# Squares of three norms: added by GpSimd two tiles at a time, then two products with ones instead of eight

## What is computed

```
def rmsnorm(x, w):
    xf = x.astype(jnp.float32)
    y = xf * lax.rsqrt(jnp.mean(xf * xf, axis=-1, keepdims=True) + NORM_EPS)
    return (y * w.astype(jnp.float32)).astype(x.dtype)
...
    for i in range(DEPTH):
        h = rmsnorm(x, norm_mix[i])
        ...                                   # i = 0: gated linear attention, i = 1: attention
        x = x + conv_ffn(rmsnorm(x, norm_ffn[i]), ffn_w_up[i], ffn_w_conv[i],
                         ffn_b_conv[i], ffn_w_down[i])
    return x
```

## Time and profile before

| | us |
|---|---|
| median of 3 runs | 1097.27 (1096.15 to 1099.2) |
| the profiled execution | 1096.36 |
| its span, first to last instruction | 1094.2 |

### The profile page before, as it was taken

One profiled execution on the slowest core, in us unless ns is written; L12 is line 12 of the kernel. 1 busy time (PEld: TensorE's weight loads), 2 busy tenths in 40 slices (PEclk: granted clock), 3 DMA queues, 4 the chain that ended last, 5 costly groups with the idle time before them and its releaser, 6 DMA issues.

```text
span 1094.2 us, 25181 instructions
## 1 busy us (share of the span) xinstructions
PE 1049.2 (96%) x10822; PEld 997.4 (91%) x10822; DVE 834.3 (76%) x1372; ACT 614.0 (56%) x878; POOL 15.4 (1%) x32
## 2 busy tenths in 40 slices
PE   3999999999998999999999978999999999999997
PEld 2999999999998988999999978889999988889997
DVE  3964579878887775997888756789899899855573
ACT  4853565444445664654444457646568576676443
POOL 1000000000000000000000000000000000000000
PEclk9999999999999999999999989999999999999999
DMA  8462256766654422567665744433333232224531
GB/s 271 145 203 77 78 177 222 249 234 203 222 192 154 147 85 96 173 233 246 215 229 192 214 131 126 127 98 120 114 117 117 79 117 79 79 79 153 192 118 39
DMA packets 135431, 168.08 MB, mean 154 GB/s; under 512 B 2928, under 2 KB 124784, under 8 KB 134960
## 3 DMA queue, kind: packets, MB, share of 16 engines
q1 hardware_dynamic: 131632, 153.51, 43.5%
q0 software_dynamic: 3712, 13.31, 3.2%
HBM read 164.70 MB, written 2.10 MB: 152 GB/s over the span
## 4 chain that ended last, share of the span: by engine, by line
PE 86%; DVE 8%; ACT 3%; DMA 1%; issue 1%; SPq 0%; DVEq 0%; ACTq 0%
PE bank L310 18%; PE bank L311 16%; PE bank L312 16%; PE banks L619 2%; PE bank L623 2%; PE bank L621 2%; PE banks L623 2%; PE bank L619 2%; PE banks L621 2%; DVE hf L2408 2%; DMA consts<-in_consts 1%; PE bank L1129 1%; DVE wl L272 1%; PE banks L1097 1%; DVE wl L296 1%; PE bank L582 1%
## 5 line engine op out<-in xcount | busy, mean ns | idle before, releaser
L310 PE MATMUL bank<-xh,wh 128*128 128x256 f32 x1360 | 398.5, 293 | 0.6 <-DVE wl L272 0.6
L311 PE MATMUL bank<-xl,wh 128*128 128x256 f32 x1392 | 393.8, 283 | 0.0
L312 PE MATMUL bank<-xh,wl 128*128 128x256 f32 x1360 | 384.6, 283 | 0.0
L310 PEld LDWEIGHTS bank<-xh,wh 128*128 128x128 f32 x1360 | 260.1, 191 | 11.1 <-issue 4.1
L311 PEld LDWEIGHTS bank<-xl,wh 128*128 128x128 f32 x1392 | 266.7, 192 | 1.1 <-issue 1.0
L312 PEld LDWEIGHTS bank<-xh,wl 128*128 128x128 f32 x1360 | 260.3, 191 | 0.0
L272 DVE TENSOR_TENSOR wl<-raw,wh 128x2048 fp32r<-128x2048 f32 x96 | 218.9, 2286 | 50.3 <-ACT wh L267 50.1
L267 ACT ACTIVATE wh<-raw 128x2048 fp32r<-128x2048 f32 x96 | 182.8, 1906 | 38.6 <-PE bank L623 34.3
L296 DVE TENSOR_TENSOR wl<-raw,wh 128x1024 fp32r<-128x1024 f32 x86 | 103.7, 1217 | 23.2 <-ACT wh L288 23.1
L2408 DVE SCALAR_TENSOR_TENSOR hf<-big,vecs,hf 128x256 f32<-128x256 f32 x240 | 101.4, 477 | 0.0
L288 ACT ACTIVATE wh<-raw 128x1024 fp32r<-128x1024 f32 x86 | 87.6, 1057 | 11.2 <-PE bank L312 5.5
(11 more groups left out here) (394 smaller groups left out, 2207.1 us busy)
## 6 DMA issues: line engine op xcount, KB each, us to landing
raw<-in_ffn_w_up SPq DMA_DIRECT2D x44, 1024.0 KB, 5.1
raw<-in_w_in SPq DMA_DIRECT2D x36, 1024.0 KB, 5.5
raw<-in_ffn_w_down SPq DMA_DIRECT2D x22, 1024.0 KB, 5.1
raw<-in_gla_w_in SPq DMA_DIRECT2D x12, 1024.0 KB, 6.1
big<-in_ada_w_t POOLq DMA_DIRECT2D x24, 512.0 KB, 5.4
raw<-in_attn_w_qkv SPq DMA_DIRECT2D x6, 1024.0 KB, 5.0
raw<-in_gla_w_out SPq DMA_DIRECT2D x4, 1024.0 KB, 5.0
raw<-in_attn_w_out SPq DMA_DIRECT2D x4, 1024.0 KB, 5.1
```

The costliest lines, as they stand in the source:

```text
L310: nc.tensor.matmul(ps, wh, xh, start=start, stop=False)
L311: nc.tensor.matmul(ps, wh, xl, start=False, stop=False)
L312: return nc.tensor.matmul(ps, wl, xh, start=False, stop=stop)
```

## The change

For the three norms GpSimd adds the squares of the pairs 1, 2 and 3 to those of pair 0 in `HF[:, 0:2, :]`, one pair as soon as ACT has written it, each addition waiting for the one before. TensorE no longer issues ones products in m = 0 of `early_product`. It waits for the third addition behind the second group of three matmuls of m = 1 and there issues two products with ones. GpSimd's queue holds the additions of norm 1 ahead of the first modulation load, those of norm 2 ahead of load 12, and those of norm 3 ahead of load 14.

```
+            def squares_added(i):
+
+                for g in range(1, 4):
+                    pool.wait_ge(sem("squares_ready"), 4 * i + g + 1)
+                    if g > 1:
+                        pool.wait_ge(sem("squares_added"), 3 * (i - 1) + g - 1)
+                    ins = nc.gpsimd.tensor_tensor(HF[:, 0:2, :], HF[:, 0:2, :], HF[:, 2 * g:2 * g + 2, :], ALU.add)
+                    ins.then_inc(sem("squares_added"), 1)
+
             pool.wait_ge(sem("rms_split"), 4)
             pool.wait_ge(sem("gla_out_split"), GH_)
+            squares_added(1)
             pool.wait_ge(sem("rstd_ready"), 2)
             for j in range(MODS):
+                if j == MODS_FIRST:
+                    squares_added(2)
+                    pool.wait_ge(sem("attn_split"), QH)
+                if j == MODS_FIRST + 2:
+                    squares_added(3)
                 if j >= 3:
                     pool.wait_ge(sem("ada_summed"), j - 2)
-                if j == MODS_FIRST:
-                    pool.wait_ge(sem("attn_split"), QH)
...
-                        if m == 0 and k % 2:
-                            pe.wait_ge(sem("squares_ready"), 4 * i + k // 2 + 1)
-                            for kk in (k - 1, k):
-                                summed = nc.tensor.matmul(PS[3][:, 0:T], ones, HF[:, kk, :], start=kk == 0,
-                                                          stop=kk == KT - 1)
-                            if k == KT - 1:
-                                summed.then_inc(sem("square_sums"), 1)
+                        if m == 1 and k == 1:
+                            pe.wait_ge(sem("squares_added"), 3 * i)
+                            for kk in range(2):
+                                summed = nc.tensor.matmul(PS[3][:, 0:T], ones, HF[:, kk, :], start=kk == 0, stop=kk == 1)
+                            summed.then_inc(sem("square_sums"), 1)
```

## The result

The changed kernel took 1102.34 us (median of 5 runs, 1100.28 to 1103.97), the kernel before, run beside it, 1096.15 (1094.51 to 1099.2). The ratio is 1.0043, with a 95% interval of 1.0028 to 1.0057, so 4.7 us (3.1 to 6.2) are lost. The two medians are 6.2 us apart, and the measured one lies 2.3 us above the forecast; for gains and losses I go by the ratios and their intervals. The forecast was 2.75 us of loss, 1100.0 us, with a range of 1093.3 to 1104.5 that holds the measured time. The profiled execution has a span of 1100.2 us against 1094.2, 6.0 us more. I first give where these 6.0 lie; the experiments then show that two of the places need a second look.

The account below looks back on a forecast made before the run. TensorE was taken as the bound in norm 1, VectorE close behind or tight in the others. Losses of 0.15, 0.4 and 2.2 us made 2.75, added to the median 1097.3: 1100.0 us, range 1093.3 to 1104.5.

Parts of the forecast that it names:

- Turns decide: All three norms: GpSimd additions and VectorE's two-input SBUF instructions exclude each other; 2.75 us slower in sum, chance 0.48.
- starvation: Norms 1 and 3: GpSimd gets no turn while VectorE runs back to back; 6.9 us slower in all, chance 0.14.
- Rival 1: All three norms: the additions disturb nobody, VectorE's instructions keep their lengths; 3.7 us faster, chance 0.27.
- An addition: Duration of one GpSimd addition: 1.25 us, the middle by ratio of VectorE's 0.68 and 2.29 us.
- The second estimate: Duration of one GpSimd addition from the skill's ratio of 1.96 between GpSimd and VectorE: given as 1.35 us.
- GpSimd's wake: GpSimd starts late after the semaphore it waits for: 0.6 us.
- Norm 1: First norm: the third addition delays VectorE's splits by 1.25 us less 0.26 idle; the down product starts 0.15 us later.
- the free case: GpSimd disturbs nobody: gains of 1.1, 2.5 and 0.1 us in norms 1, 2 and 3, sum 3.7 us.
- Norm 2: Second norm: low parts alternate with additions, the last ending at 356.8 instead of 353.88; the product ends 0.4 us later.
- TensorE waits for VectorE in that stretch anyway: Norm 2, window 353 to 354 at 1.2 GHz: counted without cost; up to 2.9 us if it lasted through m = 1.
- Norm 3: Third norm: the three additions push VectorE by 2.35 us; the down product starts 2.2 us later.
- rival 3: Additions over 1.8 us, or 1.2 GHz through norm 2: 1 to 2 us on top of either case; chance 0.11.

Follow-up runs that it names:

- a2: The kernel before with the nine GpSimd additions beside it, written to spare tiles, TensorE keeping all its products; ratio 1.0029 to the kernel before, 3.2 us slower.
- a3: The changed kernel with GpSimd copying pairs of squares to spare tiles instead of adding, sums over pair 0 alone; ratio 0.9985 to the kernel before.
- a4: The changed kernel with GpSimd writing zeros to spare tiles instead of adding, sums over pair 0 alone; ratio 0.9975 to the kernel before.
- a1: The changed kernel without the additions, sums over pair 0 alone; ratio 0.9976 to the kernel before, 2.6 us faster.
- d1: The changed kernel with six of eight ones products put back into each norm as filling, additions kept; ratio 1.0032 to the kernel before.

## Why the prediction was right, and where it was not

- **Turns decide (the choice that no row proved).** Right, and shown by a2, a3 and a4. The engine that asks first is served at the end of the other's instruction; starvation is refuted, since the addition at 158.31 came while VectorE ran back to back, took 1.47 us, was served ahead of the splits, and RS was not late in norm 1. Rival 1, no disturbance, is refuted by a2.
- **An addition.** 1.25 us forecast, 1.28 measured, up to 2.69 with its own wait in it. The second estimate there, 0.68 x 1.96, is 1.33 and not 1.35; nothing hangs on it. GpSimd's wake was taken as 0.6 us from a DMA issue; in norms 2 and 3 the additions started 0.1 us after the squares.
- **Norm 1.** +0.15 forecast, 0.0 measured. The two splits grew by 1.10, and TensorE waited 0.68 us for the hidden tiles, as the prediction said it would. The gain of 1.1 in the free case was right too (a1: 25.36).
- **Norm 2.** +0.4 forecast against the earlier trace rows, +0.38 measured against the same rows. The agreement is luck, since two sizes were wrong and cancel. TensorE was to start pair 3 at 356.86 - 350.07 = 6.79 us into the norm, and started it after 5.95, as pair 1, which the prediction put off by a whole addition, was not held up at all. Behind it 4.46 us were to follow, and 5.30 did, the first part of them at 0.50:

```profile
358.89 0.58 PE L310 MATMUL bank<-early_hi,wh 128*128 128x256 f32 x1 [0.17 <-DVE early_lo L1920]
```

The baseline flatters too: the step "TensorE waits for VectorE in that stretch anyway" took the window at 0.50 as costless. It had cost 1.6 us of the 10.87. At equal clock the additions alone cost 10.51 - 9.25 = 1.3 us (a2), and without a drop the saving is 0.84 and not 2.5.
- **Norm 3.** +2.2 forecast, +2.76 measured. The turns alone are smaller than the forecast: +1.84 in a2 and +2.01 in d1, since early_lo's low parts grew by 0.2 + 1.65 and not by 2.35. The other 0.8 to 0.9 is the clock, which the sum had only for norm 2. TensorE made the sums at 1.2 GHz, and VectorE ran out of work for 0.69 us. VectorE, ScalarE and TensorE there after:

```profile
448.57 3.41 DVE L1920 SCALAR_TENSOR_TENSOR early_lo<-x,vecs,early_hi 128x256 fp32r<-128x256 f32 x4
451.91 4.48 DVE L272 TENSOR_TENSOR wl<-raw,wh 128x2048 fp32r<-128x2048 f32 x2
457.08 1.67 DVE L1907 SCALAR_TENSOR_TENSOR hf<-x,vecs,rs 128x256 f32<-128x256 f32 x4 [0.69 <-ACT rs L1309]
...
456.63 0.42 ACT L1309 ACTIVATE rs<-rs 128x256 f32<-128x256 f32 x1
...
454.17 1.91 PE L596 MATMUL bank<-hf,consts 128*128 128x256 f32 x4
```

The four low parts took 3.41 against 1.77. The four records of the sums took 1.91 us against 1.03 in the earlier trace rows.

The prediction also looked for new idle time of TensorE in front of the down products of norms 1 and 3. Norm 1 has it. In norm 3 of the change TensorE waits three times for a low part, 0.83, 1.35 and 0.85 us, and from the last of these waits on it runs to the down product without any. So there TensorE, slowed by the clock, was the last to be late, 0.3 us behind the hidden tiles. Without a drop, in a2, it does wait for them. First the last wait and the hidden tiles' low part of the change, then the down product of a2:

```profile
452.04 0.38 PE L310 MATMUL bank<-early_hi,wh 128*128 128x256 f32 x1 [0.85 <-DVE early_lo L1920]
...
474.47 0.69 DVE L2014 TENSOR_TENSOR gl<-big,gh 128x512 fp32r<-128x512 f32 x1 [0.76 <-ACT gh L1369]
```

```profile
474.35 0.35 PE L632 MATMUL banks<-gh,wh 128*128 128x256 f32 x1 [0.52 <-DVE gl L2017]
```

Had VectorE not stood idle for its 0.69 us, the hidden tiles would have been ready at 474.47, and norm 3 would have taken 28.4 us (an estimate), as in a2.

- **The sum.** 2.75 forecast; 3.1 in the norms against the first trace of before and 4.8 against the second. The ratios say 4.7 (3.1 to 6.2) and, again, 3.1 (1.4 to 4.7). The mechanism and the sign were right. The turns were put too high, by 0.4 us in norm 3 and 0.8 in norm 2, and the term that was missing is the clock in norm 3, in norm 2 and in the baseline of norm 2. The "clock on top of turns" of rival 3, with some 1102 us, is thus nearest to what happened, though it was put in norm 2 alone.

## What to carry to other kernels

Before work is moved to GpSimd, list what VectorE runs beside it: where that reads two tiles from SBUF, each GpSimd instruction that reads SBUF costs VectorE up to its own length, so the move pays only where VectorE has slack there. Look up the clock in the rows that a sum takes as its baseline, and take a second trace of the kernel before, because a stretch at 1.2 GHz in it turns into a gain on paper. And don't count in full the time that is freed on TensorE in a stretch where it waits for another engine: here part of it became longer waits, and part of it seems to have gone to the clock.

## What the runs showed of the hardware that I had not expected

- Drops of the granted clock to 0.50 amount to 1.7 or 3.4 us each (the sum of 1 - clock over the windows), at a few fixed places of this kernel: near 37 us, in norms 2 and 3, near 650 us. What one costs depends on the waits beside it: 1.7 cost 1.6 us in norm 2 of the kernel before, 0.1 in norm 3 of a4 and nothing in norm 2 of a3 and a4. Whether one came near 37 us differed between two traces of the same program (before: none, then 3.4 us), and moved everything behind it by 2 to 4 us.
- A copy of 128x512 takes GpSimd 0.61 us alone, an addition 1.28, a memset 0.525, and the copy holds VectorE's two-input instructions up although it has one input.
